# Two feed forwards rearranged: sums of weights on VectorE, the root applied at the down tiles, parts of 8, 6 and 8 units

## The reference, cut to what matters

```python
def rms_norm(x, g):
    y = xf * lax.rsqrt(jnp.mean(xf * xf, axis=-1, keepdims=True) + RMS_EPS)
    return (y * g).astype(x.dtype)

def swiglu(h, w_gu, w_down):              # D = 1024, F = 2816
    g, u = jnp.split(h @ w_gu, 2, axis=-1)
    return (jax.nn.silu(g) * u) @ w_down

for layer in range(2):                    # first block
    h = h + mixer(...)
    h = h + swiglu(rms_norm(h, f_norm[layer]), f_w_gu[layer], f_w_down[layer])
...
mod = silu(c) @ w_ada + b_ada             # second block: six vectors of 1024
x = x + g2 * ((silu(h @ w_gate) * (h @ w_up)) @ w_down)
```

## Time and profile before

| | us |
|---|---|
| median of 3 runs | 2130.14 |
| lowest and highest | 2129.48, 2130.19 |
| the profiled execution | 2130.11 |
| its span | 2128.3 |
| PE busy | 2069.9 (97%) |
| DVE busy | 1404.5 (66%) |
| ACT busy | 908.0 (43%) |
| POOL busy | 822.3 (39%) |
| mean granted TensorE clock | 0.995 |

### The profile page before, as it was taken

How to read it: one execution, slowest core, us unless ns; L and a number is a source line. 1 busy time by engine, 2 the same in 40 slices (tenths; PEclk the granted TensorE clock), 3 DMA queues, 4 the chain that set the end, 5 groups by cost and what they waited for, 6 DMA issues and landing times.

```text
span 2128.3 us, 29907 instructions
## 1 busy us (share of the span) xinstructions
PE 2069.9 (97%) x11578; PEld 1709.8 (80%) x11578; DVE 1404.5 (66%) x1985; ACT 908.0 (43%) x1435; POOL 822.3 (39%) x572
## 2 busy tenths in 40 slices
PE   8999999999999999999999989999999999999999
PEld 6888788989788544878898978776778888989898
DVE  6446969767464797488793956475674748739383
ACT  4124215434322688322442445554454435425352
POOL 5546853343542311475424243323223240242333
PEclk9999999999999999999999999999999999999999
DMA  5224443231532000354323231211111122233232
GB/s 174 97 99 168 162 174 119 70 126 61 193 120 72 21 1 1 129 178 160 137 83 116 76 129 44 75 60 51 49 60 60 60 80 80 90 110 107 84 115 92
DMA packets 37857, 206.53 MB, mean 97 GB/s; under 512 B 4448, under 2 KB 5600, under 8 KB 18400
## 3 DMA queue, kind: packets, MB, share of 16 engines
q1 hardware_dynamic: 35712, 197.89, 27.3%
q10 hardware_dynamic: 2016, 6.88, 1.0%
HBM read 200.63 MB, written 2.10 MB: 95 GB/s over the span
## 4 chain that ended last, share of the span: by engine, by line
PE 54%; issue 22%; POOL 12%; DVE 8%; ACT 2%; DMA 2%; SPq 0%; POOLq 0%; DVEq 0%; ACTq 0%
PE PS L751 13%; POOL WL L557 7%; PE PS L691 5%; PE PS L693 5%; PE PS L692 5%; PE PS L821 4%; PE PS L822 4%; PE PS L823 4%; POOL WL L620 3%; DVE LS L2321 2%; PE PS L1038 2%; PE PS L1069 2%; PE PS L1051 2%; DVE HF L2356 1%; POOL HN L609 1%
## 5 line engine op out<-in xcount | busy, mean ns | idle before, releaser
L557 POOL TENSOR_TENSOR WL<-WR,WH 128x512 fp32r<-128x512 f32 x224 | 310.0, 1415 | 552.6 <-ACT WH L1469 552.6
L691 PE MATMUL PS<-Hh,WH 128*128 128x512 f32 x704 | 280.7, 399 | 18.8 <-DVE Hl L2150 7.6
L692 PE MATMUL PS<-Hl,WH 128*128 128x512 f32 x704 | 277.0, 393 | 0.0
L693 PE MATMUL PS<-Hh,WL 128*128 128x512 f32 x704 | 276.9, 393 | 0.0
L1469 ACT ACTIVATE WH<-WR 128x2048 fp32r<-128x2048 f32 x73 | 139.5, 1911 | 248.8 <-PE PS L693 206.0
L636 POOL TENSOR_TENSOR LS<-WR,HS 128x512 fp32r<-128x512 f32 (+1 forms) x112 | 138.1, 1254 | 207.0 <-ACT HS L1624 207.0
L595 POOL TENSOR_TENSOR LF<-LF,WR 128x512 f32<-128x512 f32 x47 | 68.4, 1456 | 332.6 <-PE PS L751 206.8
L691 PEld LDWEIGHTS PS<-Hh,WH 128*128 128x128 f32 x704 | 133.9, 190 | 52.3 <-issue 11.0
L692 PEld LDWEIGHTS PS<-Hl,WH 128*128 128x128 f32 x704 | 134.2, 191 | 28.7 <-issue 1.0
L821 PE MATMUL PS<-G3h,HS 128*128 128x512 f32 x400 | 156.2, 390 | 0.7 <-DVE G3l L2364 0.7
L693 PEld LDWEIGHTS PS<-Hh,WL 128*128 128x128 f32 x704 | 134.0, 190 | 28.5
(11 more groups left out here) (374 smaller groups left out, 4759.6 us busy)
## 6 DMA issues: line engine op xcount, KB each, us to landing
WR<-wA SPq DMA_DIRECT2D x125, 1024.0 KB, 4.9
AW<-wada SPq DMA_DIRECT2D x24, 1024.0 KB, 4.9
WR<-wD SPq DMA_DIRECT2D x48, 512.0 KB, 3.6
WR<-wE SPq DMA_DIRECT2D x24, 384.0 KB, 3.1
X<-x_in SPq DMA_DIRECT2D x8, 256.0 KB, 6.8
W1K<-w1k ACTq DMA_DIRECT2D x1, 2048.0 KB, 8.1
W1V<-w1v ACTq DMA_DIRECT2D x1, 2048.0 KB, 12.9
out<-X SPq DMA_DIRECT2D x8, 256.0 KB, 3.7
```

The lines of the kernel that those rows point to most:

```text
L557: ins = nc.gpsimd.tensor_tensor(WL[:, s, piece], WR[:, s, piece], WH[:, s, piece].bitcast(F32), ALU.subtract)
L691: nc.tensor.matmul(PS[:, b, :], wh[:, c, cols], pe_h, start=c == 0, stop=False)
L692: nc.tensor.matmul(PS[:, b, :], wh[:, c, cols], pe_l, start=False, stop=False)
L693: last = nc.tensor.matmul(PS[:, b, :], wl[:, c, cols], pe_h, start=False, stop=c == seg.chunks - 1)
```

## The change

It touches the first two feed forwards, and the places of the down weights in all three.

- Sums two and four of the weights go from GpSimd to VectorE in layers 0 and 1 (sum_two, sum_four), so that GpSimd has no work in their parts b and c but the down weights' low parts.
- The up path is not multiplied by the root any more; the down tiles' results are, as the root is one factor a token. A new helper, rooted, makes SG = PS x RSF and then X = X + SG in place of X = X + PS.
- The parts have 8, 6 and 8 units in the first two feed forwards. Part b's down tiles have 6 chunks (18 matmuls), part c's 8 (24 matmuls). Before it was 8 in b and 6 in c.
- HN is made by ScalarE from X and the gain, behind the conversions of units 3 and 4.
- Modulation units run one hidden unit later, and five instead of four of them in the down part; their loads are moved in SP's queue.
- Down weights get more places (three in part a, four in b and c, instead of two), so that some tiles' weights are converted earlier: down_free lists what each waits for.
- The sums of the first unit of part b are no more split around the last down tiles.

```diff
-    ("gu0a", "A", 8), ("dn0a", "D", 8), ("gu0b", "A", 8), ("dn0b", "D", 8), ("gu0c", "A", 6), ("dn0c", "E", 8),
+    ("gu0a", "A", 8), ("dn0a", "D", 8), ("gu0b", "A", 6), ("dn0b", "E", 8), ("gu0c", "A", 8), ("dn0c", "D", 8),
...
+        def down_free(l, part, m):
+
+            t = SEGS[f"dn{l}{part}"].tile0
+            if part == "a" and l < 2:
+                return tile_s, (t - 2, t, t, t + 2, t + 1, t + 4, t + 3, t + 6)[m]
+            n = units_of(l, part)[-1]
+            return ((made_s, made(n - 1, P3)), (made_s, made(n, P3)), (made_s, made(n, P5)), (tile_s, t), (tile_s, t + 1),
+                    (tile_s, t + 2), (tile_s, t + 3), (tile_s, t + 6))[m]
...
-                    segment_with_ada(name, 12 * int(name[2]), {0: 1, 1: 1, 2: 3, 3: 4, 4: 5, 5: 6, 6: 7})
+                    segment_with_ada(name, 12 * int(name[2]), {0: 1, 1: 2, 2: 3, 3: 4, 4: 5, 5: 6, 6: 7})
...
-                    segment_with_ada(name, 12 * int(name[2]), {7: 0, 8: 1, 9: 2, 10: 4, 11: 5})
+                    segment_with_ada(name, 12 * int(name[2]), {7: 0, 8: 2, 9: 4, 10: 5, 11: 6})
...
-                    if u in (2, 3):
-                        whole_inputs(l, 4 * (u - 2))
...
+                elif name[0:3] in ("gu0", "gu1"):
+                    continue
...
-                if m >= 2:
-                    act.wait_ge(tile_s, seg.tile0 + m - 1)
-                elif part == "a" and l < 2:
-                    act.wait_ge(tile_s, seg.tile0 - 2 + 2 * m)
...
+                act.wait_ge(*down_free(l, part, m))
...
+                    if u in (1, 2):
+                        for m in range(4 * u - 4, 4 * u):
+                            act.wait_ge(tile_s, seg.tile0)
+                            nc.scalar.activation(HN[l][:, m, :], X[:, m, :], ACT.Copy,
+                                                 scale=pcol(("f_norm0", "f_norm1")[l], m)).then_inc(sh_s, 1)
...
+            def rooted(seg, m):
+
+                t = seg.tile0 + m
+                dve.wait_ge(evac_s, max(t - 1, seg.tile0))
+                chain.mark(nc.vector.tensor_tensor(SG[:, m % 2, :], PS[:, m % NB, :], RSF[:, :], ALU.mult))
+                chain.wait()
+                return nc.vector.tensor_tensor(X[:, m, :], X[:, m, :], SG[:, m % 2, :], ALU.add).then_inc(evac_s, 1)
...
+            def sum_two(n):
+
+                raw, sums = WR[:, slot(n), :].rearrange("p (q m) -> p q m", q=4), LF[slot(n)]
+                dve.wait_ge(s13_s, n + 1)
+                if nth(n) == 1:
+                    dve.wait_ge(tile_s, TILES_AFTER[seven_unit(n) - 2])
+                nc.vector.tensor_tensor(sums[:, W_S2, :], sums[:, W_S1, :], raw[:, A11, :], ALU.add).then_inc(s2_s, 1)
+
+            def sum_four(n):
+
+                raw, sums = WR[:, slot(n), :].rearrange("p (q m) -> p q m", q=4), LF[slot(n)]
+                dve.wait_ge(s2_s, n + 1)
+                dve.wait_ge(tile_s, TILES_AFTER[seven_unit(n) - 2])
+                nc.vector.tensor_tensor(sums[:, W_S4, :], sums[:, W_S2, :], raw[:, A12, :], ALU.add).then_inc(s4_s, 1)
...
                 dve.wait_ge(sg_s, hidden(n) + 1)
-                if layer(n) < 2:
-                    chain.mark(nc.vector.tensor_tensor(SG[:, n % 2, :], SG[:, n % 2, :], RSF[:, :], ALU.mult))
-                    chain.wait()
...
                         sums_one_three(first)
+                        if l < 2:
+                            sum_two(first)
+                    if first is not None and m == 6:
+                        if l < 2:
+                            sum_four(first)
                         quarters_low(first)
...
                     dve.wait_ge(sg_s, 22 * l + u + 1)
-                    chain.mark(nc.vector.tensor_tensor(SG[:, k, :], SG[:, k, :], RSF[:, :], ALU.mult))
-                    chain.wait()
...
-                    modulation_unit(12 * l + u, u)
+                    if u:
+                        modulation_unit(12 * l + u - 1, u - 1)
...
-                down_part(l, "a", FIRST[l], (1, 2, 4, 5))
+                down_part(l, "a", FIRST[l], (0, 2, 3, 4, 5))
...
-                residual(f"dn{l}c", next_h=next_h, both=both, lows={DC - 1: 1} if l == 1 else {})
+                residual(f"dn{l}c", next_h=next_h, both=both, lows={DC - 1: 1} if l == 1 else {}, root=True)
```

More of the change, by code:

```diff
@@ L87 @@
 PLAIN = 3
-PARTS = [("a", 8), ("b", 8), ("c", 6)]
-SEVEN = [(SEGS[f"gu{l}{part}"], k) for l in range(3) for part, n in PARTS for k in range(n)
+PARTS = "abc"
+SEVEN = [(SEGS[f"gu{l}{part}"], k) for l in range(3) for part in PARTS for k in range(SEGS[f"gu{l}{part}"].units)
          if (part != "a" if l < 2 else part != "a" or k >= PLAIN)]
@@ L140, in slot, with second_of_part @@
     return seven_unit(n) % 2
+def second_of_part(n):
+    return SEVEN[n][1] == 1 and SEVEN[n][0].name not in ("gu0b", "gu1b")
 def first_free(n):
@@ L1412, in last_feed_forward @@
                 plain_units()
-                for part, _ in PARTS:
+                for part in PARTS:
                     seven_part(2, part)
@@ L2386, in down_part @@
                         sums_one_three(first)
-                    if late and m == 6:
-                        sums_low(first, W_S3, h13_s, l13_s)
-                    elif first is not None and m == 6:
+                        if l < 2:
[3 more added lines that the diff above has]
+                            sum_four(first)
                         quarters_low(first)
```

61 lines of the change are left out of this document (29 added, 32 removed), and 2 rows, old and new, of the table SEGMENTS.

## The result

The changed kernel takes 2108.74 us (median of four runs, 2106.68 to 2109.97), the kernel before 2130.16 beside it (2129.48 to 2130.32): a ratio of 0.990, 95% interval 0.988 to 0.992, 21.4 us less. Forecast were 2100.5 us in a range of 2094 to 2110.

A forecast was written before the change was run, and what follows sets the result against it. VectorE, stretched by GpSimd, was taken to bound the early feed forwards' seven-product parts, with GpSimd in part a's chain of waits. Gains of 16.2 + 8.0 + 2.0 + 2.2 + 1.2 = 29.6 us off 2130.11 gave 2100.5, range 2094 to 2110.

The forecast's parts named there:

- the turn: Seven-product parts: VectorE's work per unit falls from 10.78 to 9.43 us, so TensorE's 10.08 us becomes the bound.
- parts b and c together: Both early feed forwards: 2 x (6.90 + 3.50) us regained less 4.6 for openings, 16.2 us gained.
- The ring: Follow-up theory, seven-product parts with GpSimd's sums: VectorE and TensorE each wait for the other once a turn, 10.78 us.
- four terms of my turn: VectorE's turn: less 0.82 (root product), 0.86 (gate product), 1.07 us (low parts), plus 1.4 for two sums and waits.
- The openings: Starts of four seven-product parts: VectorE's backlog makes up sums late, 1.15 us a part, 4.6 us lost.
- Down part a: First down part: earlier weight places gain 1.0 us a layer, 2.0 for both, bounds -0.5 and 1.5.
- Rival 1: Seven-product parts: VectorE's stretch isn't GpSimd's doing or returns; turn 11.36 us, total 2131.7 or 2136; 4 in 100.
- Part a: First part: units 3 and 4 in time, unit 6 about 1.3 us late; 4.0 us gained a layer, 8.0 total.
- The ends: Ends of both early feed forwards: shorter waits gain 2.2 us in the first and 1.2 in the second.
- Rival 2: Part a: its waits only move to unit 6, 8 us less gain, total 2108.5; 15 in 100.
- rival 3: Last down tiles: X + SG held behind GpSimd's down weights, four openings each lose 2 us more; 2108; 8 in 100.
- my own forecast: Whole kernel: 29.6 us gained, 2100.5 us; 60 in 100 for between 2098 and 2105.

The follow-up runs named there:

- the run with three orders: Changed kernel with adaLN loads one place later, unit 6 converted before unit 4's silu, and root values copied before the fourth sum's high parts: 2102.35 us.
- e2_mod_back: Changed kernel with the modulation units and their loads back in their old places: 2106.37 us, ratio 0.989 to the kernel before.
- e8_up_first: Changed kernel with sums two and four back on GpSimd and VectorE's up sums ahead of its gate sums: 2110.35 us.
- e10_open: The run with three orders plus, in the openings, unit 0's up sums before gate sums and quarters' low parts before the fourth sum: 2102.31 us.

## Why the prediction was right, and where not

**Right: the turn.** Work of 9.51 us against 9.43 forecast, TensorE the bound at 10.08, the fourth sum's wait of 0.42 us; parts b and c together 16.3 us less, for 16.2. Three things in its reasoning need a correction.

- I charged VectorE alone with the old turn of 10.78 because nothing in it was idle. The ring is in it too: TensorE waited 0.44 us for U (358.33), and VectorE's gate product began 0.82 us after the instruction before it (359.32 and 360.14, a slot of 0.61), just when TensorE's last up product was done. VectorE's own work was then about 10.57 us (estimate: 10.78 less 0.21), still over TensorE's 10.08. So by this count another order alone could have given back 0.2 us of the old turn; no run tried it. The 10.09 us of the run with the up sums first had the root product out as well.
- The 0.82 us of the removed product, one of the four terms of my turn, is worth nothing in these parts by itself: with GpSimd's sums left where they were the turn stayed at 10.78, and with the sums on VectorE it costs 0.1 us a turn, which the parts' lengths don't show. The two returned stretches (1.9 us) are what made the room.
- The openings, 4.6 us forecast, measured 4.2: 0.95 and 1.10 us over TensorE's 59.03 and 79.19 in the first feed forward, 1.0 and 1.1 in the second. For part b the agreement is luck. I had 1.15 us behind a down part a at nearly full pace; it came behind one that was 2.9 us longer than its matmuls, in which VectorE caught up. Behind a full down part it is 2.57 us (61.60 us, the run with three orders). Down part a and b together were forecast at 104.1 us; in the first feed forward the changed kernel took 106.38, and 106.35 to 106.51 in the runs with HN on GpSimd, with the loads later and with the modulation back.

Rival 1 is excluded, the stretch is GpSimd's doing: it returned with GpSimd's sums (2.85 and 1.28 us).

**Part a: 6.3 us instead of 8.0.** The 5.3 us of losses were read rightly (the rows of what is left, below, add up to the same base of about 88.0 us); I forecast 4.0 of them gained a layer, and 3.1 and 3.3 came. The waits at units 3 and 4 went, and the granted clock went to 1.00. What is left is 2.2 us instead of 1.3: unit 6 is 1.49 us late, with 0.1 us of restart, unit 5 0.46 with its restart (241.42), and 0.16 come at unit 7. The cause was also named too narrowly: putting HN back costs 1.3 and 1.5 us, putting the root back 6.2 and 3.6, so of the edits the root's move matters more in this part. They aren't additive, and I priced one. How much of the 1.6 us of slow clock HN's move took away is open, as the same wait was not always followed by it.

**Down part a: the step that failed.** I forecast 1.0 us gained a layer and wrote that tile 1's load might be late, with a bound of 0.5 lost. It is 1.24 us late, tile 7's 1.31: the part lost 1.5 and 1.3 us, 4.8 us from the forecast in both. That is over half of the miss of 8.2. The sentence had the mechanism, and the price was never worked out, though the rows of SP's queue and of the modulation units were there to start from. The runs with the loads later show one more thing, that the part's gain is mostly returned to the opening behind it, because VectorE does the modulation, the doubled residual and the opening's sums in one stretch. Only with loads, conversion and copy changed together did a gain stay (6.4 us by the medians, 3.6 by the profiled executions); the loads and the conversion were tried alone, no two of the three together.

**The ends: 1.5 us instead of 3.4.** Waits of 2.64 and 6.08 us for 4.37 and 7.24 of before are gains of 1.7 and 1.2, near the forecast. But the stages lost again what I had put at nothing with "b has 6 and c 8 units now changes no total". The down part b has two waits of 0.4 us. The one for VectorE's last G3l (387.69) isn't new, the six-chunk down part c had it before (523.10). The other stands before the last tile:

```profile
410.08 3.27 POOL L645 TENSOR_TENSOR LS<-WR,HS 128x384 fp32r<-128x384 f32 x2 [7.90 <-ACT HS L1631]
...
413.41 0.50 PE L832 MATMUL PS<-G3h,HS 128*128 128x512 f32 x1 [0.26 <-POOL LS L645]
```

ScalarE converts the last tile's weights at 409.16, when the tile two before is done, and a tile of six chunks (4.1 us) no longer covers conversion and low parts (4.2 us). With the restart this costs 0.55 us a layer, 1.1 in both. Another 0.4 us came behind the second end's wait, where the statistics products take 6.57 us instead of 6.18, the last of them 0.85 instead of 0.64. X + SG was held, as forecast from the earlier trace rows:

```profile
1236.25 3.70 DVE L2244 TENSOR_TENSOR X<-X,SG 128x512 f32<-128x512 f32 x1
...
1234.67 4.73 POOL L564 TENSOR_TENSOR WXL<-WR,WXH 128x2048 fp32r<-128x2048 f32 x1 [0.29 <-ACT WXH L1472]
```

Rival 2 gave nearly the measured time (2108.5) for another reason, its stretch of VectorE's work at unit 6 (5.3 us late) isn't there; of rival 3 only a part came: the doubled residual, held or not, costs 0.9 and 1.8 us at the ends, in the run with the root in its old place. The medians agree with rival 2, the trace with my own forecast less the down part, the ends and 1.7 us of part a. What stays open: why stages that no edit touches differ by up to 3 us between executions, of which TensorE's clock is one part (below).

## What to carry to other kernels

A turn can be longer than the work of either engine in it: add up the way from one handover to the next, look for a ring with the partner, and try the order before the load. A move must be followed through every queue that it feeds; here a load that waits for a moved step held the weights of the next stage, and fixing one engine's order alone made the kernel 11 us slower, while the same edit with the loads moved belongs to the two fastest versions (2102.3 us). Work taken to an idle GpSimd isn't free for VectorE if both read SBUF. Between two kernels that differ by 2 us, compare the stages that an edit touches and those that it doesn't.

## What the runs showed of the hardware

VectorE and GpSimd both pay when they overlap: a product of 1.22 us took 2.32, low parts of 1.76 took 2.85, an X + SG of 0.69 took 1.65 (303.06 in the run with the openings' sums on GpSimd) and 3.70, and GpSimd's sum of 1.30 took 2.74. In these rows the excess follows GpSimd's instruction beside it: up to 1.1 us beside pieces of 512 columns, 3.0 us beside the one of 2048. In the last case the X + SG began 1.6 us after GpSimd's instruction (1236.25 and 1234.67) and ended at 1239.95, 0.55 us after it (1239.40), as if it had run when the other was done. The Trainium skill ("SBUF — State Buffer", Who interferes with whom) says that a VectorE instruction with two SBUF inputs contends with a GpSimd instruction that reads SBUF, and calls the pair of ports that they share an exclusive lock. The rows agree, and by them a long GpSimd instruction in small pieces would bound what one wait can cost.

The length of TensorE's wait alone doesn't tell whether its granted clock falls behind it. After 1.33 us idle (253.93) and after 1.81 us (243.17, HN on GpSimd) the matmuls went on at 0.23 us; after 1.83 us in the earlier trace rows and 2.64 us at 545.73 some seven came to stand 0.43 apart (1.2 of 2.4 GHz), and not the first ones behind the wait. TensorE's rows behind the 2.64 us:

```profile
546.53 0.40 PE L702 MATMUL PS<-Hh,WH 128*128 128x512 f32 x1
546.77 0.53 PE L703 MATMUL PS<-Hl,WH 128*128 128x512 f32 x1
547.10 0.63 PE L704 MATMUL PS<-Hh,WL 128*128 128x512 f32 x1
```

The same wait of 2.63 to 2.64 us ahead of the same matmuls had no slow one behind it in three other runs (e2_mod_back, e8_up_first, e10_open). The 11.01 us behind it in the changed kernel and in e10_open (PEclk is the third number from the end):

```profile
545.73:556.74 11.01, 11.01 (x41) 8.94 (x42) 2.37 (x4) 1.90 (x2) 5.24 (x4) 0.85 0.52 174
...
543.39:554.40 11.01, 11.01 (x48) 9.12 (x49) 2.37 (x4) 1.91 (x2) 5.27 (x4) 1.00 0.52 170
```

The first holds seven matmuls less, which is the 1.6 us by which this stage differs between runs. With the root after silu again, a wait of 2.84 us in the first feed forward had thirteen slow matmuls behind it (granted clock 0.72 over the next 10.9 us) and one of 2.74 us in the second none (1.00). What decides it, these runs don't show.
